# A third slot for the split weights of the first step behind three LayerNorms, and the order of work around it

## The chip, the cores and the metric

The kernel runs on one core of a Trainium2 chip. The metric is the device time of one execution in microseconds (us). The engines, as the profile names them, are PE (TensorE, matrix products; PEld is its weight load), DVE (VectorE), ACT (ScalarE), POOL (GpSimd) and SP (SyncE, which here only issues DMAs). Each engine runs its own instruction list in order, and semaphores join the lists.

## The reference

Two decoder layers on 512 tokens of width 1024. Each layer is a mixer and a gated MLP, each followed by a LayerNorm over the residual sum:

```python
for i in range(DEPTH):                       # DEPTH = 2
    if i % 2 == 0:
        m = even_mixer(x, w_qkv_ab[i // 2], w_o_ab[i // 2], cos, sin)
    else:
        m = odd_mixer(x, w_qkv_c[i // 2], w_o_c[i // 2])
    x = layer_norm(DEEPNORM_ALPHA * x + m, ln_mix_g[i], ln_mix_b[i])
    f = conv_ffn(x, w_up[i], conv_w[i], conv_b[i], w_down[i])
    x = layer_norm(DEEPNORM_ALPHA * x + f, ln_ffn_g[i], ln_ffn_b[i])
```

`even_mixer` and `odd_mixer` are two kinds of attention, each with a q/k/v product before and an output product behind it. `conv_ffn` is `u = h @ w_up` (1024 to 2 x 2816), a causal convolution of width 3, `silu(g) * val`, and `@ w_down` (2816 to 1024). All is float32.

## The kernel before

**Products in three parts.** Every large product is made from a high and a low part of both factors: hi x hi, hi x lo and lo x hi are added in a PSUM bank. ACT copies a rounded high part, and the low part is the difference. So each weight takes three operations: SP loads it into `w_raw`, ACT writes `w_hi` (`heads`, L267, or half a step at a time in `unit_heads`, L274), and POOL writes `w_lo = w_raw - w_hi` in two units (`rest`, L215).

**Weight steps.** The weights are a stream of 98 steps of 1 MB, 49 for each layer: 0 is q and k of the first attention position, 1 to 4 are v, 5 to 11 are q and k of the other positions, 12 to 15 the output product, 16 to 37 the MLP's first product, 38 to 48 its second. Step c uses slot c % 2 of `w_raw`, `w_hi` and `w_lo`. Hence ACT may write the high part of step c only when PE has finished step c - 2, which `heads` waits for on the semaphore `w_used`. POOL's end of step c (`lo_ready`) lets PE use it, and lets SP load step c + 2.

**A LayerNorm.** There are four, numbered i = 0 to 3; behind the first three comes a product that needs the result turned (transposed), with its columns along the partitions. The 512 tokens are four tiles t of 128 rows, and tile t owns the banks 2t and 2t + 1. PE ends the product in front tile by tile (`last_two`). For tile t, DVE adds the bank to the residual and takes the mean (`norm_sum`, L537, L542); ACT takes the variance (`norm_stats`, L290 to L296); DVE makes (x - mean) * gain in `ln_mul` (`norm_mul`, L553), four tiny operations on [128x1] (`norm_out`, L561, L564, L567, L569) and the result in `x` (L572), which raises `xn`. Then PE turns the tile with eight transposes (`turn_x`, L775) back into the tile's banks, ACT writes its high part (`xt_heads`, L283) and DVE its low part (`xt_rests`, L525), which raises `lo`.

**Who turns what, when.** PE turns tile 0 and tile 1 between the last four visits of the product in front. Tile 2 is turned after its end. Then `first_columns` runs the first step behind the LayerNorm: its two units on the tokens of tiles 0 and 1 (24 matmuls each), then `turn_x` of tile 3, then other work (`meanwhile`), then both units on tiles 2 and 3. The other work is the same half of the next step (`up_half`, i = 0 and 2), or one tile of the first v step, 12 matmuls (`v_meanwhile`, i = 1). Steps 16, 49 and 65 are the first ones behind LayerNorm 0, 1 and 2.

**Memory.** The buffers of the attention, of the MLP and of the LayerNorm lie in the same stretch, one over another, since they are not alive at once. ACT loads `tri` (a mask of the second layer's attention) behind LayerNorm 1.

The only loops in this part are the ones over steps far from the LayerNorms. The order is written out by hand on each engine.

## Time and profile before

| | us |
|---|---|
| median of 3 runs | 1278.67 |
| lowest, highest | 1278.08, 1280.11 |
| the profiled execution, whole time | 1279.5 |
| its span, first to last instruction | 1277.7 |
| PE busy in the span | 1225.5 |
| ACT, DVE, POOL busy | 506.8, 639.3, 548.0 |

The span and what lies around it make up the profiled execution's own time, which is 0.8 us above the median. Times below are counted from the start of the span. A row of the timeline gives start, duration, engine, line, operation, and out<-in; in brackets stand the idle time before it and who ended it. A matmul's duration is longer than the spacing of matmuls, which are pipelined.

### The profile page before, as it was taken

The page shows a single profiled execution, that of the slowest core. Times are in us where ns is not written, and L with a number is a line of the kernel's source. Part 1 is how long each engine was busy: PE and PEld are TensorE (multiplying, and loading weights), DVE is VectorE, ACT ScalarE, POOL GpSimd, SP SyncE. Part 2 cuts the span into 40 slices and gives each one's busy share as a digit, 9 for nine tenths or more (in the row PEclk, how much of TensorE's full clock was granted, in tenths as well). Part 3 has the DMA queues.
Part 4 walks back from the last instruction along what each step waited for, and adds up shares of the span by engine and source line. Part 5 has one row for each costly group of instructions (what it writes and reads, how often), then busy time and mean ns, then how long its engine had stood idle before and what let it go on. Part 6 is the DMA issues. An engine that isn't in the chain of part 4 may idle for free.

```text
span 1277.7 us, 17006 instructions
## 1 busy us (share of the span) xinstructions
PE 1225.5 (96%) x6224; PEld 1008.6 (79%) x6224; DVE 639.3 (50%) x1007; ACT 506.8 (40%) x749; POOL 548.0 (43%) x240
## 2 busy tenths in 40 slices
PE   7999998989999999999989999989899999999996
PEld 7877776779888888888778777768888888888885
DVE  2036565285566656522370465553676565552226
ACT  3236465344333333322232456643443333343222
POOL 5535353333444444455434333312364444444551
PEclk9999999989999999999989999999999999999998
DMA  7221222122222222222222111111222222222211
GB/s 287 99 84 58 90 69 81 66 92 107 92 91 88 93 96 98 99 98 98 99 101 100 66 66 66 48 52 66 100 99 98 98 98 98 98 98 99 98 66 66
DMA packets 19879, 117.25 MB, mean 92 GB/s; under 512 B 2433, under 2 KB 2817, under 8 KB 7425
## 3 DMA queue, kind: packets, MB, share of 16 engines
q1 hardware_dynamic: 18256, 112.21, 24.5%
q10 hardware_dynamic: 1584, 4.51, 1.0%
q8 instruction: 28, 0.46, 0.1%
q14 instruction: 11, 0.08, 0.0%
HBM read 110.41 MB, written 2.10 MB: 88 GB/s over the span
## 4 chain that ended last, share of the span: by engine, by line
PE 57%; issue 23%; POOL 10%; DVE 6%; ACT 3%; DMA 0%; POOLq 0%; ACTq 0%; SPq 0%; DVEq 0%
PE bank L829 32%; PE bank L799 18%; POOL w_lo L215 10%; PE bank L875 2%; PE bank L902 1%; PE bank L889 1%; DVE probs L677 1%; PE bank L959 1%; DVE x L572 1%; PE bank L940 1%; PE bank L948 1%; ACT w_hi L267 1%; PE bank L775 1%; DVE x L537 1%; DMA x<-x_in 0%
## 5 line engine op out<-in xcount | busy, mean ns | idle before, releaser
L215 POOL TENSOR_TENSOR w_lo<-w_raw,w_hi 128x1024 fp32r<-128x1024 f32 x196 | 504.3, 2596 | 634.8 <-ACT w_hi L267 577.2
L829 PE MATMUL bank<-xt_hi,w_hi 128*128 128x512 f32 (+1 forms) x1056 | 399.2, 378 | 1.7 <-ACT v_all L304 1.7
L829 PE MATMUL bank<-xt_lo,w_hi 128*128 128x512 f32 (+1 forms) x1056 | 398.8, 378 | 0.0
L829 PE MATMUL bank<-xt_hi,w_lo 128*128 128x512 f32 (+1 forms) x1056 | 394.7, 374 | 0.0
L267 ACT ACTIVATE w_hi<-w_raw 128x2048 fp32r<-128x2048 f32 x94 | 179.6, 1911 | 206.6 <-PE bank L799 206.6
L829 PEld LDWEIGHTS bank<-xt_hi,w_hi 128*128 128x128 f32 x1056 | 201.3, 191 | 38.8 <-ACT v_all L304 2.4
L829 PEld LDWEIGHTS bank<-xt_lo,w_hi 128*128 128x128 f32 x1056 | 201.1, 190 | 38.9 <-issue 4.8
L829 PEld LDWEIGHTS bank<-xt_hi,w_lo 128*128 128x128 f32 x1056 | 201.0, 190 | 33.6
L799 PE MATMUL bank<-w_hi,a_hi 128*128 128x512 f32 x480 | 151.7, 397 | 2.9 <-POOL w_lo L215 1.9
L799 PE MATMUL bank<-w_hi,a_lo 128*128 128x512 f32 x480 | 148.8, 391 | 0.0
L799 PE MATMUL bank<-w_lo,a_hi 128*128 128x512 f32 x480 | 148.6, 391 | 0.0
L751 DVE TENSOR_TENSOR a_lo<-h_all,a_hi 128x1024 fp32r<-128x1024 f32 x22 | 52.9, 2405 | 150.1 <-ACT a_hi L462 150.1
L743 DVE TENSOR_TENSOR h_all<-sig,cv 128x512 f32 (+1 forms) x44 | 119.1, 2706 | 6.1 <-DVE cv L733 0.2
L799 PEld LDWEIGHTS bank<-w_hi,a_hi 128*128 128x128 f32 x480 | 88.8, 188 | 25.1 <-POOL w_lo L215 4.3
L799 PEld LDWEIGHTS bank<-w_hi,a_lo 128*128 128x128 f32 x480 | 90.3, 188 | 19.3 <-issue 0.2
L799 PEld LDWEIGHTS bank<-w_lo,a_hi 128*128 128x128 f32 x480 | 90.3, 188 | 19.1
L471 ACT ACTIVATE cg<-bank,conv 128x512 f32<-128x512 f32 x44 | 34.2, 778 | 122.4 <-PE bank L829 122.1
L729 DVE SCALAR_TENSOR_TENSOR cv<-bank,conv,cv 128x511 f32<-128x511 f32 x44 | 33.0, 749 | 91.2 <-ACT cv L477 91.2
L477 ACT ACTIVATE cv<-bank,conv 128x512 f32<-128x512 f32 x44 | 34.2, 777 | 82.3 <-PE bank L829 82.2
L475 ACT ACTIVATE sig<-cg 128x512 f32<-128x512 f32 x44 | 27.8, 632 | 82.5 <-DVE cg L733 82.5
L729 DVE SCALAR_TENSOR_TENSOR cg<-bank,conv,cg 128x511 f32<-128x511 f32 x44 | 33.0, 749 | 46.0 <-ACT cg L471 46.0
L329 ACT ACTIVATE probs<-probs,sm 128x128 f32<-128x128 f32 (+3 forms) x64 | 35.4, 555 | 43.1 <-DVE sm L633 43.1
(87 smaller groups left out, 1159.5 us busy)
## 6 DMA issues: line engine op xcount, KB each, us to landing
w_raw<-w_stream SPq DMA_DIRECT2D x97, 1024.0 KB, 4.8
x<-x_in SPq DMA_DIRECT2D x4, 512.0 KB, 7.1
gain<-ln_in ACTq DMA_DIRECT2D x4, 512.0 KB, 4.1
shift<-ln_in ACTq DMA_DIRECT2D x4, 512.0 KB, 5.3
qs<-qc SPq DMA_DIRECT2D x16, 128.0 KB, 2.1
ks<-kc SPq DMA_DIRECT2D x16, 128.0 KB, 2.1
out<-x SPq DMA_DIRECT2D x4, 512.0 KB, 2.6
w_raw<-w_stream SPq DMA_DIRECT2D x2, 512.0 KB, 6.0
```

What stands on the lines that cost most here:

```text
L215: pool.tensor_tensor(w_lo[s][:, part], w_raw[s][:, part], w_hi[s][:, part].bitcast(F32), ALU.subtract).then_inc(lo_ready, 1)
L267: act.activation(w_hi[c % 2][:, :], w_raw[c % 2][:, :], ACT.Copy).then_inc(hi_ready, 2)
L329: act.activation(e, e, ACT.Exp, bias=m[:, 0:1], scale=-1.0, accum_out=m[:, 1:2]).then_inc(a["ex"], 1)
L471: act.activation(cg[s][:, :], bank[2 * s][:, :], ACT.Identity, bias=tap(l, f, 3), scale=tap(l, f, 2)).then_inc(u["cg"], 1)
L475: act.activation(sig[s][:, :], cg[s][:, :], ACT.Sigmoid).then_inc(u["sg"], 1)
L477: act.activation(cv[s][:, :], bank[2 * s + 1][:, :], ACT.Identity, bias=tap(l, f + KF, 3), scale=tap(l, f + KF, 2)).then_inc(u["cv"], 1)
L729: dve.scalar_tensor_tensor(out=acc[:, 1:S], in0=ps[:, 0:S - 1], scalar=tap(l, tile, 1), in1=acc[:, 1:S], op0=ALU.mult, op1=ALU.add).then_i ...
L743: dve.tensor_tensor(h_all[:, bass.ds(f, 1), :], sig[s][:, :].rearrange("p (a q) -> p a q", a=1), cv[s][:, :].rearrange("p (a q) -> p a q", ...
L751: dve.tensor_tensor(a_lo[:, k:k + 2, :], h_all[:, bass.ds(2 * j, 2), :], a_hi[:, k:k + 2, :].bitcast(F32), ALU.subtract).then_inc(DN[l]["a ...
L799: mm = pe.matmul(bank[2 * t + g][:, :], lhs, w[s][:, u * UNIT + g * HALF:u * UNIT + (g + 1) * HALF], start=first and n == 0, stop=end and ...
L829: mm = pe.matmul(out_bank[:, tok], w, m, start=n == 0, stop=n == len(todo) - 1)
L875: mm = pe.matmul(bank[2 + h][:, k * P:(k + 1) * P], qa[par][part, qi * P:(qi + 1) * P], ka[par][part, k * P:(k + 1) * P], start=True, stop ...
```

## The change

Three steps, 16, 49 and 65, get slot 2 of `w_hi` and `w_lo`; the others count on in slots 0 and 1 without them. `w_raw` keeps two slots. The new buffers `w_hi2` and `w_lo2` lie above the LayerNorm's buffers, over buffers of attention and MLP that are dead by then; `cg1`, `cv1` and `sig1` are moved up, and the load of `tri` is moved behind the use of step 49. On the engines: ACT writes the high part of these steps ahead of the LayerNorm's first statistics; DVE's `xt_rests` of tiles 0 and 1 come earlier; PE no longer turns tile 2 ahead of the first step behind, but after its first unit, and tile 3 one half unit later than before.

```diff
@@ -50,6 +50,14 @@
+AHEAD = (AT_UP, PER_LAYER, PER_LAYER + AT_UP)
...
+def slot(c):
+    return 2 if c in AHEAD else (c - sum(a < c for a in AHEAD)) % 2
@@ -101,13 +109,16 @@
-            cg = [sb(f"cg{s}", [P, S], stack=st) for s in range(2)]
-            cv = [sb(f"cv{s}", [P, S], stack=st) for s in range(2)]
-            sig = [sb(f"sig{s}", [P, S], stack=st) for s in range(2)]
+            cg, cv, sig = ([sb(f"{n}0", [P, S], stack=st)] for n in ("cg", "cv", "sig"))
+            sb("below_second", [P, S], stack=st)
+            for n, tiles in (("cg", cg), ("cv", cv), ("sig", sig)):
+                tiles.append(sb(f"{n}1", [P, S], stack=st))
...
+            w_hi.append(sb("w_hi2", [P, 2 * UNIT], F32R, stack=st))
+            w_lo.append(sb("w_lo2", [P, 2 * UNIT], F32R, stack=st))
@@ -212,8 +223,8 @@
-                    pool.tensor_tensor(w_lo[s][:, part], w_raw[s][:, part],
-                                       w_hi[s][:, part].bitcast(F32), ALU.subtract).then_inc(lo_ready, 1)
+                    pool.tensor_tensor(w_lo[slot(c)][:, part], w_raw[s][:, part],
+                                       w_hi[slot(c)][:, part].bitcast(F32), ALU.subtract).then_inc(lo_ready, 1)
@@ -251,9 +262,11 @@
-                with pool.Fori(0, (PER_LAYER - AT_UP) // 2) as it:
+                rest(b + AT_UP)
+                rest(b + AT_UP + 1)
+                with pool.Fori(0, (PER_LAYER - AT_UP - 2) // 2) as it:
...
-                        rest(b + AT_UP + j, it)
+                        rest(b + AT_UP + 2 + j, it)
@@ -264,14 +277,7 @@
-                act.activation(w_hi[c % 2][:, :], w_raw[c % 2][:, :], ACT.Copy).then_inc(hi_ready, 2)
...
-            def unit_heads(c, u):
...
-                act.wait_ge(raw_full[c % 2], filled(c, 0))
-                act.wait_ge(w_used, c - 1)
-                part = slice(u * UNIT, (u + 1) * UNIT)
-                act.activation(w_hi[c % 2][:, part], w_raw[c % 2][:, part], ACT.Copy).then_inc(hi_ready, 1)
+                act.activation(w_hi[slot(c)][:, :], w_raw[c % 2][:, :], ACT.Copy).then_inc(hi_ready, 2)
@@ -430,12 +436,11 @@
-                    act.wait_ge(N[1]["xn"], NT)
-                    act.dma_start(tri[:, :], tri_in).then_inc(tri_full, 16)
...
+                    act.dma_start(tri[:, :], tri_in).then_inc(tri_full, 16)
@@ -451,6 +456,7 @@
                     heads(b + AT_O + 2 + c)
+                heads(b + AT_UP, used=False)
                 for i, after in ((2 * l, b + AT_O + 4), (2 * l + 1, b + PER_LAYER)):
@@ -497,6 +503,8 @@
                                 chunk_heads(j + 2, it)
+                        if l < DEPTH - 1:
+                            heads(after, used=False)
                     if i == 2 * DEPTH - 1:
@@ -505,10 +513,9 @@
-                        unit_heads(after, 0)
...
-                        unit_heads(after, 1)
-                        heads(after + 1)
+                        act.wait_ge(w_used, after - 1)
+                        heads(after + 1, used=False)
@@ -581,11 +588,12 @@
                 norm_sum(i, 2)
+                if turn:
+                    xt_rests(i + 1, 0)
                 norm_mul(i, 2)
                 if turn:
-                    xt_rests(i + 1, 0)
+                    xt_rests(i + 1, 1)
                     norm_out(i, 2)
-                    xt_rests(i + 1, 1)
                     norm_sum(i, 3)
@@ -783,15 +791,15 @@
-                    c, it, slot = steps[m]
-                    s = c % 2
+                    c, it, at = steps[m]
+                    s = slot(c)
...
-                        hi = a[0][:, slot + u, t * P:(t + 1) * P]
-                        lo = a[1][:, slot + u, t * P:(t + 1) * P]
+                        hi = a[0][:, at + u, t * P:(t + 1) * P]
+                        lo = a[1][:, at + u, t * P:(t + 1) * P]
@@ -816,7 +824,7 @@
-                s = c % 2
+                s = slot(c)
@@ -840,9 +848,12 @@
                             pass
+                        if (half, unit) == (0, 0) and i > 0:
+                            turn_x(i, 2)
                     if half == 0 and i > 0:
+                        meanwhile(0)
                         turn_x(i, 3)
-                        meanwhile()
+                        meanwhile(1)
@@ -995,6 +1006,8 @@
                 def first_v(t, _):
+                    if t >= 2:
+                        pe.wait_ge(T[2 * l]["lo"], 2 * t + 2)
                     if t == 0:
@@ -1006,7 +1019,7 @@
-                def v_meanwhile():
+                def v_meanwhile(_):
@@ -1042,11 +1055,10 @@
-                turn_x(2 * l + 1, 2)
@@ -1054,17 +1066,17 @@
-                def up_half(half):
...
-                    for unit in range(2):
-                        for _ in col_unit(b + AT_UP + 1, 0, unit, bank[2 + unit], U[l]["g_mm"], half):
-                            pass
...
-                first_columns(b + AT_UP, 0, U[l]["g_mm"], 2 * l + 1, lambda: up_half(0))
-                up_half(1)
-                with pe.Fori(1, KF // 2) as it:
-                    up_body(0, it)
-                    up_body(1, it)
+                def up_half(half, unit):
...
+                    for _ in col_unit(b + AT_UP + 1, 0, unit, bank[2 + unit], U[l]["g_mm"], half):
+                        pass
...
+                first_columns(b + AT_UP, 0, U[l]["g_mm"], 2 * l + 1, lambda unit: up_half(0, unit))
+                up_half(1, 0)
+                up_half(1, 1)
+                with pe.Fori(0, KF // 2 - 1) as it:
+                    up_body(2, it)
+                    up_body(3, it)
@@ -1091,8 +1103,6 @@
-                if l < DEPTH - 1:
-                    turn_x(2 * l + 2, 2)
```

**ACT at the start of LayerNorm 0** (`w_hi0` is slot 0 of the high parts, `n0_` and `t1_` semaphores of LayerNorm 0 and of the turning behind it), before and then after:

```order
L267 ACTIVATE w_hi0<-w_raw0 128x2048 [waits w_used,raw_full0]
L267 ACTIVATE w_hi1<-w_raw1 128x2048 [waits w_used,raw_full1]
L290 ACTIVATE ln_junk,stat<-x,stat 128x1024 [waits n0_mean]
L293 ACTIVATE stat<-stat,eps 128x1 [waits n0_sq]
```

```order
L280 ACTIVATE w_hi0<-w_raw0 128x2048 [waits w_used,raw_full0]
L280 ACTIVATE w_hi1<-w_raw1 128x2048 [waits w_used,raw_full1]
L280 ACTIVATE w_hi2<-w_raw0 128x2048 [waits raw_full0]
L296 ACTIVATE ln_junk,stat<-x,stat 128x1024 [waits n0_mean]
L299 ACTIVATE stat<-stat,eps 128x1 [waits n0_sq]
```

The high part of step 16 now stands ahead of the first variance, in slot 2, and waits only for its load.

**ACT in the middle of LayerNorm 0**, from the variance of tile 2 on, before and then after:

```order
L290 ACTIVATE ln_junk,stat<-x,stat 128x1024 [waits n0_mean]
L293 ACTIVATE stat<-stat,eps 128x1 [waits n0_sq]
L296 ACTIVATE stat<-stat 128x1 [waits n0_lv]
L274 ACTIVATE w_hi0<-w_raw0 128x1024 [waits w_used,raw_full0]
L283 ACTIVATE xt_hi<-bank2 128x4x128 [waits t1_mm]
L283 ACTIVATE xt_hi<-bank3 128x4x128
L274 ACTIVATE w_hi0<-w_raw0 128x1024 [waits w_used,raw_full0]
L267 ACTIVATE w_hi1<-w_raw1 128x2048 [waits w_used,raw_full1]
```

```order
L296 ACTIVATE ln_junk,stat<-x,stat 128x1024 [waits n0_mean]
L299 ACTIVATE stat<-stat,eps 128x1 [waits n0_sq]
L302 ACTIVATE stat<-stat 128x1 [waits n0_lv]
L289 ACTIVATE xt_hi<-bank2 128x4x128 [waits t1_mm]
L289 ACTIVATE xt_hi<-bank3 128x4x128
L280 ACTIVATE w_hi0<-w_raw1 128x2048 [waits raw_full1,w_used]
```

The two half steps of 16 are gone; step 17 stays behind `xt_heads` of tile 1, as one whole step.

**DVE at the same place**, from the mean of tile 2 on, before and then after:

```order
L542 TENSOR_SCALAR stat<-stat 128x1 [waits n0_sum]
L553 SCALAR_TENSOR_TENSOR ln_mul<-x,stat,gain 128x1024 [waits n0_xn,n0_mean]
L525 TENSOR_TENSOR xt_lo<-bank0,xt_hi 128x4x128 [waits t1_hi]
L525 TENSOR_TENSOR xt_lo<-bank1,xt_hi 128x4x128
L561 TENSOR_SCALAR stat<-stat 128x1 [waits n0_sq]
L564 SCALAR_TENSOR_TENSOR stat<-stat 128x1 [waits n0_y0,n0_va]
L567 TENSOR_SCALAR stat<-stat 128x1 [waits n0_nt]
L569 TENSOR_TENSOR stat<-stat 128x1 [waits n0_nt]
L572 SCALAR_TENSOR_TENSOR x<-ln_mul,stat,shift 128x1024 [waits n0_mulg,n0_nt]
L525 TENSOR_TENSOR xt_lo<-bank2,xt_hi 128x4x128 [waits t1_hi]
L525 TENSOR_TENSOR xt_lo<-bank3,xt_hi 128x4x128
```

```order
L549 TENSOR_SCALAR stat<-stat 128x1 [waits n0_sum]
L532 TENSOR_TENSOR xt_lo<-bank0,xt_hi 128x4x128 [waits t1_hi]
L532 TENSOR_TENSOR xt_lo<-bank1,xt_hi 128x4x128
L560 SCALAR_TENSOR_TENSOR ln_mul<-x,stat,gain 128x1024 [waits n0_xn,n0_mean]
L532 TENSOR_TENSOR xt_lo<-bank2,xt_hi 128x4x128 [waits t1_hi]
L532 TENSOR_TENSOR xt_lo<-bank3,xt_hi 128x4x128
L568 TENSOR_SCALAR stat<-stat 128x1 [waits n0_sq]
L571 SCALAR_TENSOR_TENSOR stat<-stat 128x1 [waits n0_y0,n0_va]
L574 TENSOR_SCALAR stat<-stat 128x1 [waits n0_nt]
L576 TENSOR_TENSOR stat<-stat 128x1 [waits n0_nt]
L579 SCALAR_TENSOR_TENSOR x<-ln_mul,stat,shift 128x1024 [waits n0_mulg,n0_nt]
```

The low parts of tiles 0 and 1 (L525, now L532) both stand ahead of the four tiny operations and of the result of tile 2 (L572, now L579).

**PE at the end of step 15**, before, and then the two places after where step 16 begins and where tile 2 is turned:

```order
L799 MATMUL bank6<-w_hi1,a_lo 128x512
L799 MATMUL bank7<-w_hi1,a_lo 128x512
L775 MATMUL bank4<-ident,x 128x128 [waits n0_xn]
L775 MATMUL bank4<-ident,x 128x128 x3
L775 MATMUL bank5<-ident,x 128x128 x4
L829 MATMUL bank0<-xt_hi,w_hi0 128x256 [waits lo_ready,t1_lo]
L829 MATMUL bank0<-xt_lo,w_hi0 128x256
```

```order
L807 MATMUL bank6<-w_hi1,a_lo 128x512
L807 MATMUL bank7<-w_hi1,a_lo 128x512
L837 MATMUL bank0<-xt_hi,w_hi2 128x256 [waits lo_ready,t1_lo]
L837 MATMUL bank0<-xt_lo,w_hi2 128x256
L837 MATMUL bank0<-xt_hi,w_lo2 128x256
```

```order
L837 MATMUL bank0<-xt_lo,w_hi2 128x256
L837 MATMUL bank0<-xt_hi,w_lo2 128x256
L783 MATMUL bank4<-ident,x 128x128 [waits n0_xn]
L783 MATMUL bank4<-ident,x 128x128 x3
L783 MATMUL bank5<-ident,x 128x128 x4
L837 MATMUL bank1<-xt_hi,w_hi2 128x256 [waits lo_ready]
L837 MATMUL bank1<-xt_lo,w_hi2 128x256
```

Tile 2's turn (banks 4 and 5, waiting for `n0_xn`) has moved behind the 24 matmuls of the first unit (bank 0). Tile 3's turn (banks 6 and 7) moved likewise behind the first half unit of step 17.

## Rows read from the trace of the kernel before

**Rows 1.** The page: PE busy in the span, and the DMA issues of the weights.

```profile
PE 1225.5 (96%) x6224; PEld 1008.6 (79%) x6224; DVE 639.3 (50%) x1007; ACT 506.8 (40%) x749; POOL 548.0 (43%) x240
...
w_raw<-w_stream SPq DMA_DIRECT2D x97, 1024.0 KB, 4.8
```

**Rows 2.** PE's waits: engine line, waited for: us in total, times, longest.

```profile
PE bank L775 <- DVE x L572: 13.6, 3, 4.5
```

**Rows 3.** Timeline of PE at LayerNorm 0: start us, us, engine, line, operation.

```profile
273.74 0.62 PE L799 MATMUL bank<-w_lo,a_hi 128*128 128x512 f32 x2
274.19 0.61 PE L799 MATMUL bank<-w_hi,a_lo 128*128 128x512 f32 x2
279.31 1.97 PE L775 MATMUL bank<-ident,x 128*128 128x128 f32 x8 [4.51 <-DVE x L572]
...
288.40 1.03 PE L775 MATMUL bank<-ident,x 128*128 128x128 f32 x8
289.19 0.36 PE L829 MATMUL bank<-xt_hi,w_hi 128*128 128x256 f32 x1
289.39 0.28 PE L829 MATMUL bank<-xt_lo,w_hi 128*128 128x256 f32 x1
289.51 0.28 PE L829 MATMUL bank<-xt_hi,w_lo 128*128 128x256 f32 x1
```

**Rows 4.** Timeline of PE at LayerNorms 1 and 2, turns of tiles 2 and 3.

```profile
652.28 1.97 PE L775 MATMUL bank<-ident,x 128*128 128x128 f32 x8 [4.55 <-DVE x L572]
...
660.96 1.03 PE L775 MATMUL bank<-ident,x 128*128 128x128 f32 x8
...
901.80 1.40 PE L775 MATMUL bank<-ident,x 128*128 128x128 f32 x8 [4.50 <-DVE x L572]
...
910.10 1.04 PE L775 MATMUL bank<-ident,x 128*128 128x128 f32 x8
```

**Rows 5.** Timeline of DVE at LayerNorm 0.

```profile
260.99 1.28 DVE L553 SCALAR_TENSOR_TENSOR ln_mul<-x,stat,gain 128x1024 f32<-128x1024 f32 x1
...
271.86 1.28 DVE L525 TENSOR_TENSOR xt_lo<-bank,xt_hi 128x512 fp32r<-128x512 f32 x2
...
273.68 2.21 DVE L569 TENSOR_TENSOR stat<-stat 128x1 f32<-128x1 f32 x1
...
275.93 3.33 DVE L572 SCALAR_TENSOR_TENSOR x<-ln_mul,stat,shift 128x1024 f32<-128x1024 f32 x1
...
281.95 2.96 DVE L553 SCALAR_TENSOR_TENSOR ln_mul<-x,stat,gain 128x1024 f32<-128x1024 f32 x1
...
290.59 1.29 DVE L525 TENSOR_TENSOR xt_lo<-bank,xt_hi 128x512 fp32r<-128x512 f32 x2 [2.46 <-ACT xt_hi L283]
```

**Rows 6.** Timeline of ACT at LayerNorm 0.

```profile
272.38 1.04 ACT L274 ACTIVATE w_hi<-w_raw 128x1024 fp32r<-128x1024 f32 x1
273.32 1.06 ACT L283 ACTIVATE xt_hi<-bank 128x512 fp32r<-128x512 f32 x2
...
275.23 1.91 ACT L267 ACTIVATE w_hi<-w_raw 128x2048 fp32r<-128x2048 f32 x1
```

**Rows 7.** Timeline of POOL at LayerNorm 0, and at step 51.

```profile
252.88 4.75 POOL L215 TENSOR_TENSOR w_lo<-w_raw,w_hi 128x1024 fp32r<-128x1024 f32 x2 [3.41 <-ACT w_hi L267]
273.50 10.34 POOL L215 TENSOR_TENSOR w_lo<-w_raw,w_hi 128x1024 fp32r<-128x1024 f32 x4 [15.86 <-ACT w_hi L274]
...
673.04 4.73 POOL L215 TENSOR_TENSOR w_lo<-w_raw,w_hi 128x1024 fp32r<-128x1024 f32 x2 [16.25 <-ACT w_hi L267]
```

**Rows 8.** Stretches: length, busy us (instructions) of each engine, PE clock, DMA.

```profile
279.30:284.60 5.30, 5.29 (x25) 5.29 (x26) 5.23 (x8) 2.58 (x6) 4.53 (x2) 0.50 0.54 198
...
844.40:847.80 3.40, 3.40 (x10) 2.62 (x9) 2.42 (x5) 1.61 (x4) 0.69 (x1) 0.50 0.41 116
...
850.10:854.00 3.90, 2.32 (x14) 2.07 (x15) 3.80 (x6) 1.65 (x4) 0.00 (x0) 1.00 0.00 0
```

**Rows 9.** Timeline of PE: waits of the odd attention ahead of two stretches of rows 8.

```profile
843.66 0.33 PE L948 MATMUL bank<-ident,probs 128*128 128x128 f32 x1 [2.48 <-ACT probs L380]
...
851.68 0.55 PE L948 MATMUL bank<-ident,probs 128*128 128x128 f32 x3 [1.59 <-ACT probs L380]
```

## The prediction

> **What bounds the kernel now.** The page comes first: PE is busy 1225.5 of 1277.7 us [rows 1], so a gain must come from PE's idle time or from its clock. PE's waits come next. The longest entry is the turning of tiles (L775), which waits three times for DVE's LayerNorm result (L572), 13.6 us in all [rows 2]: 4.51 us at LayerNorm 0 [rows 3], 4.55 and 4.50 at LayerNorms 1 and 2 [rows 4]. Each is the turn of tile 2, placed where PE has nothing else to do.
>
> The timeline then shows two things behind these waits. First, a wait costs a little more than its idle time: matmuls are issued every 0.227 us (rows of two, 0.45 apart), so PE could have issued again at 274.19 + 0.45 = 274.64 but issued at 279.31 [rows 3]. That is 4.67, or idle + 0.16; for the others 4.71 and 4.66. Second, the clock: the granted clock stands at 0.50, the lower level of 1.2 GHz, right behind the wait [rows 8]. From the turn of tile 2 to that of tile 3 PE has 8 transposes (288.40 to 289.19 = 0.79) and 48 matmuls (0.12 each, 289.39 to 289.51), 6.55 us at full clock; it took 288.40 - 279.31 = 9.09 [rows 3], 8.68 and 8.30 [rows 4]. The clock cost 2.54, 2.13 and 1.75. Together: 14.04 + 6.42 = **20.5 us** stand behind these three turns.
>
> Why does L572 come so late? POOL subtracts steps 16 and 17 from 273.50 to 283.84 [rows 7]. While it runs, DVE's operations with two inputs in SBUF stand: L569 on [128x1] takes 2.21 us, L572 takes 3.33 where 1.28 is its usual time (as that of L553 at 260.99), L553 at 281.95 takes 2.96 and ends 1.07 behind POOL's last subtraction [rows 5, 7]. L569 caught the first subtraction (2.38 us each, half of 4.75) and L572 the second.
>
> **The change, part by part,** at LayerNorm 0; the other two run the same pattern.
>
> *The high part of step 16 goes first.* Its load is issued when the subtraction of step 14 ends (ahead of 252.88) and lands 4.8 us later [rows 1], long before POOL is free at 252.88 + 4.75 = 257.63 [rows 7]. So POOL subtracts step 16 from 257.6 to 262.35. That meets L553 of tile 0, issued at 260.99: it ends at 262.35 + 1.07 = 263.42, not 262.27. DVE's chain is **late by 1.15 us** from there. PE doesn't feel it at the turns of tiles 0 and 1, which by my reading stand 1.6 and 1.9 us behind their results in the trace.
>
> *The first unit no longer waits for tile 2.* It needs both low parts of tiles 0 and 1. ACT's variance of tile 2 ended for its next operation at 272.38 [rows 6]; 1.15 later is 273.53. There stands now `xt_heads` of tile 1, with no half step ahead of it: done 1.06 later, 274.59 [rows 6]. DVE follows in 0.04 and takes 1.29 for the low part [rows 5]: 275.92; PE issues at about 275.96. Lost: 275.96 - 274.64 = **1.32 us**. DVE reaches that point with 0.4 us to spare, so its new order costs nothing.
>
> *Tile 2 is turned after 24 matmuls.* PE is ready at 275.96 + 24 x 0.12 = 278.84. When is `x` there? L569 starts 1.82 us behind the first subtraction of a low part (271.86 to 273.68 [rows 5]), at 274.63 + 1.82 = 276.45; L572 is due 0.2 us later. On ACT the high part of step 17 starts 0.95 behind `xt_heads` (273.32 to 274.28, by its own length less the overlap), at 274.48, takes 1.91 [rows 6] and POOL starts 0.08 behind it (273.42 to 273.50), at **276.47**. So L569 and POOL start within 0.02 us of each other, which my arithmetic can't separate. Two answers:
> - DVE is first. L569 is through at once, POOL takes over at about 276.6 and L572 stands for one subtraction: 276.6 + 2.38 + 1.07 = 280.05. PE issues at 280.10, lost **1.26**.
> - POOL is first, as in the trace. L569 stands until 278.85, L572 until 281.2, and ends at 282.27. PE issues at 282.32, lost **3.48**.
>
> I take the first: by the sum DVE is 0.02 us ahead. In both, POOL has 2 subtractions there, not 4.
>
> *Tile 3 is turned after two more half units.* PE gets there at 280.10 + 0.79 + 48 x 0.12 = 286.65. L553 of tile 3 meets the second subtraction (to about 282.4), ends at 283.5, and L572 about 2.0 us later, 285.5. No wait, 1.1 us to spare. The low part of tile 3 is done 3.48 us after the turn begins (288.40 to 290.59 + 1.29 [rows 3, 5]); the cover was two half units and is now one: 0.79 + 24 x 0.12 = 3.67 us. It holds by 0.15 us, so I cost it at nothing; with 12 matmuls of a v tile at LayerNorm 1 the cover is 3.51, even. If the cover is gone, it costs the lateness one for one, under 0.5 us.
>
> *One new wait, at step 51.* Behind LayerNorm 1 three tiles of the first v step (8.2 us) stood between the end of step 49 and step 51; now two (5.45 us), since one went into the cover. ACT still starts step 51 only when step 49 is used, though slot 1 is free sooner, and POOL ends it at 673.04 + 4.73 = 677.77 [rows 7]. PE's half of step 49 ends at about 670.36, so its second unit is due at 670.36 + 5.45 + 1.36 = 677.17: lost 0.6, **0.65 us** with the hand-over. It could be 0 if the halves slip, and at most 2.7, the work that moved.
>
> *Loads, `tri`, slots.* SP may load step 18 at 262.4, much earlier than before, into a queue that is idle there. `tri` is needed 30 us after its new place. Slots 0 and 1 serve steps as far apart as before. Nothing here.
>
> **The clock.** No row shows two waits of 1.2 us so close. The nearest: behind a wait of 1.59 us the clock stays at 1.00, behind one of 2.48 us it stands at 0.50 [rows 8, 9]. Single waits of 1.1 us are nearer to the first, both together (2.3 idle) nearer to the second. Bounds: 0, and 2.54, 2.13, 1.75 as now. I take 0, as each wait is followed by 24 matmuls without a gap.
>
> **The sum.** Before 20.5. After 3 x (1.32 + 1.26) + 0.65 = 8.4. Gain 12.1 us: 1279.5, the profiled execution's time, becomes 1267.4; against the median, 0.8 lower, **1266.6**.
>
> **The rivals.**
> 1. *Two short waits, and the clock falls as before.* Adds 6.4: 1273.0. For it: 2.3 us idle within 5.
> 2. *POOL first, double block.* 3 x (1.32 + 3.48) + 0.65 = 15.05, and the clock falls as before, 6.42: 21.5 against 20.5, so 1279.7. For it: a margin of 0.02 us, and that all three LayerNorms show this order today. The gain is then eaten by the 1.15 and by waits that only moved.
> 3. *L572 slips in as well.* L572 is due 0.04 us behind L569's end. If it is in first, it ends at 276.65 + 1.28 = 277.93, before PE is ready: 3 x 1.32 + 0.65 = 4.6, 1262.8. Against it: POOL's third subtraction was held by L572 (10.34 us for four, 0.8 more than 4 x 2.38), and resumed with no gap that I can see; a waiting POOL took over between L569 and L572. The Trainium skill, SBUF — State Buffer, "A bandwidth-pool intuition that's wrong", has a blocked GpSimd resume about 115 ns after DVE ends; by that rule L572 would be in first and the time would be this one.
> 4. *Slower: the clock stays low for longer.* Double block as in 2, but the low clock runs over both waits and what lies between, twice the loss of now (12.8): 6.4 more, 1286. It decides once the three low stretches cost over 8 us together, 2.7 each; LayerNorm 0 stands at 2.54 today.
> 5. *The early subtraction doesn't happen,* because step 16's load or high part is late: then POOL's four subtractions stay in the middle and the time about 1279. Against: 3 us between landing and POOL's being free.
>
> Beside rivals 2 and 3: the trace shows that the one that is there first holds the other up for its whole operation (L572, 3.33 us). The Trainium skill says the same in SBUF — State Buffer, "SBUF: two separate sides": the shared port pair is an exclusive lock for "whichever … starts first". By that rule and the 0.02 us the time would be the forecast; it also speaks against this change, as it puts one more POOL step against the LayerNorm's first tile.
>
> **How the numbers follow.** Forecast 0.42; rival 1 0.14; rival 2 0.25; rival 3 0.07; rival 4 0.08; rival 5 0.04. A measurement of this kernel tells 0.2%, 2.6 us, from no change. Faster: 0.42 + 0.14 + 0.07 = 0.63. Slower: rival 4 and the upper edge of 2, 0.11. Same: 0.26. The range leaves out rivals 3 and 4: 1264 (forecast less the 0.65 and some of the waits) to 1281.5 (rival 2 with 2 us of clock). Most of the chance has one sign, yet the range must reach over no change.
>
> **What would show it.** L553 of tile 0 at about 2.4 us, not 1.28. PE's waits for L525 of 1.2 us and for L572 of about 1.0 us (or 3.3) at each LayerNorm, instead of 4.5. POOL one step of 4.75 us ahead and one in the middle. L569 at 0.16 or 2.2 us, which alone tells forecast from rival 2. Clock 1.00 or 0.50 behind the waits. A wait of PE for POOL of 0.6 us near step 51. I am wrong if POOL meets DVE elsewhere, or if PE's cover for tile 3 is short.

## The result, and the profile after

| | us |
|---|---|
| kernel before, median of 4 runs beside it | 1279.16 (1278.08 to 1280.11) |
| kernel after, median of 4 runs | 1268.04 (1266.48 to 1268.33) |
| ratio, 95% interval | 0.991 (0.990 to 0.992) |
| profiled execution of after, its span | 1268.13, 1266.2 |

The change makes the kernel 11.1 us (0.9%) faster; the forecast was 1266.6 us. The page shows first that PE does the same work in less time: 6224 matmuls as in [rows 1], busy 5.9 us less. These 5.9 us go with the clock; the other 5.6 of the span's 11.5 (1277.7 less 1266.2) are idle time.

```profile
PE 1219.6 (96%) x6224; PEld 1001.3 (79%) x6224; DVE 632.5 (50%) x1007; ACT 507.0 (40%) x746; POOL 548.3 (43%) x240
```

PE's waits (engine line, waited for: us in total, times, longest). L783, L837, L807 are L775, L829, L799 of before; L579 and L532 are L572 and L525. The 13.6 us of [rows 2] have become 3.1. In their place stand 3.7 us for the low part of tile 1. The waits for POOL were 1.9 us, 3 times, in before; the fourth, at step 51, is new:

```profile
PE bank L837 <- DVE xt_lo L532: 3.7, 3, 1.2
PE bank L783 <- DVE x L579: 3.1, 3, 1.0
PE bank L807 <- POOL w_lo L226: 2.6, 4, 0.8
```

PE's timeline has two short waits at each LayerNorm, here at LayerNorms 0, 1 and 2, where [rows 3, 4] had one of 4.5 us. The last row is step 51:

```profile
276.77 0.39 PE L837 MATMUL bank<-xt_hi,w_hi 128*128 128x256 f32 x1 [1.24 <-DVE xt_lo L532]
...
280.82 1.09 PE L783 MATMUL bank<-ident,x 128*128 128x128 f32 x8 [1.05 <-DVE x L579]
...
645.08 0.38 PE L837 MATMUL bank<-xt_hi,w_hi 128*128 128x256 f32 x1 [1.21 <-DVE xt_lo L532]
...
649.12 1.09 PE L783 MATMUL bank<-ident,x 128*128 128x128 f32 x8 [1.03 <-DVE x L579]
...
890.97 0.39 PE L837 MATMUL bank<-xt_hi,w_hi 128*128 128x256 f32 x1 [1.21 <-DVE xt_lo L532]
...
895.02 1.09 PE L783 MATMUL bank<-ident,x 128*128 128x128 f32 x8 [1.05 <-DVE x L579]
...
672.39 0.73 PE L807 MATMUL bank<-w_hi,xt_hi 128*128 128x512 f32 x2 [0.70 <-POOL w_lo L226]
```

DVE and POOL at LayerNorm 0 show who met whom. The product with the gain of tile 0 (L560) now takes 2.46 us, since POOL's early subtraction is there. L576 of tile 2 starts 0.014 us ahead of POOL (277.255 and 277.269 before rounding), and is through in 0.16 us. L579 then stands for one subtraction and takes 3.31 us:

```profile
261.76 2.46 DVE L560 SCALAR_TENSOR_TENSOR ln_mul<-x,stat,gain 128x1024 f32<-128x1024 f32 x1
...
277.25 0.16 DVE L576 TENSOR_TENSOR stat<-stat 128x1 f32<-128x1 f32 x1
277.45 3.31 DVE L579 SCALAR_TENSOR_TENSOR x<-ln_mul,stat,shift 128x1024 f32<-128x1024 f32 x1
```

```profile
253.66 9.47 POOL L226 TENSOR_TENSOR w_lo<-w_raw,w_hi 128x1024 fp32r<-128x1024 f32 x4 [3.41 <-ACT w_hi L280]
...
277.27 5.75 POOL L226 TENSOR_TENSOR w_lo<-w_raw,w_hi 128x1024 fp32r<-128x1024 f32 x2 [14.13 <-ACT w_hi L280]
```

The stretches (length, busy us and instructions of PE, PEld, DVE, ACT, POOL, then PE clock and DMA) show the clock at 1.00, the upper level of 2.4 GHz, behind the second wait; the same stretch of before stood at 0.50 [rows 8]:

```profile
279.30:284.60 5.30, 4.25 (x38) 4.06 (x37) 5.16 (x10) 2.27 (x6) 3.72 (x2) 1.00 0.11 20
```

### The profile page after: what moved, and what is told of

The parts are those of the page before. It is cut to its first block, busy times and chain, and to the rows that moved or that the text cites. A ratio compares the mean times of both kernels' runs of the same rounds, so it can differ in the third digit from the quotient of the medians.

```text
span 1266.2 us, 17008 instructions
## 1 busy us (share of the span) xinstructions
PE 1219.6 (96%) x6224; PEld 1001.3 (79%) x6224; DVE 632.5 (50%) x1007; ACT 507.0 (40%) x746; POOL 548.3 (43%) x240
## 4 chain that ended last, share of the span: by engine, by line
PE 57%; issue 23%; POOL 10%; DVE 5%; ACT 3%; DMA 1%; POOLq 0%; SPq 0%; ACTq 0%; DVEq 0%
PE bank L837 31%; PE bank L807 18%; POOL w_lo L226 10%; PE bank L886 2%; PE bank L913 1%; PE bank L900 1%; DVE probs L685 1%; PE bank L970 1%; DVE x L579 1%; PE bank L951 1%; ACT w_hi L280 1%; PE bank L959 1%; DVE x L544 1%; DMA x<-x_in 1%; DVE ln_mul L560 0%
## 5 line engine op out<-in xcount | busy, mean ns | idle before, releaser
L837 PE MATMUL bank<-xt_hi,w_hi 128*128 128x512 f32 (+1 forms) x1056 | 397.1, 376 | 5.3 <-DVE xt_lo L532 3.7
L837 PE MATMUL bank<-xt_lo,w_hi 128*128 128x512 f32 (+1 forms) x1056 | 396.6, 376 | 0.0
L837 PE MATMUL bank<-xt_hi,w_lo 128*128 128x512 f32 (+1 forms) x1056 | 392.7, 372 | 0.0
L280 ACT ACTIVATE w_hi<-w_raw 128x2048 fp32r<-128x2048 f32 x97 | 185.4, 1911 | 209.1 <-PE bank L807 204.6
L837 PEld LDWEIGHTS bank<-xt_hi,w_hi 128*128 128x128 f32 x1056 | 198.8, 188 | 43.3 <-DVE xt_lo L532 5.1
L837 PEld LDWEIGHTS bank<-xt_lo,w_hi 128*128 128x128 f32 x1056 | 198.7, 188 | 39.3 <-issue 4.8
L837 PEld LDWEIGHTS bank<-xt_hi,w_lo 128*128 128x128 f32 x1056 | 198.7, 188 | 33.4
L807 PE MATMUL bank<-w_hi,a_hi 128*128 128x512 f32 x480 | 151.9, 397 | 2.9 <-POOL w_lo L226 1.9
L807 PE MATMUL bank<-w_lo,a_hi 128*128 128x512 f32 x480 | 148.5, 391 | 0.0
L807 PE MATMUL bank<-w_hi,a_lo 128*128 128x512 f32 x480 | 148.3, 390 | 0.0
L807 PEld LDWEIGHTS bank<-w_hi,a_hi 128*128 128x128 f32 x480 | 89.0, 188 | 25.4 <-POOL w_lo L226 4.3
L807 PEld LDWEIGHTS bank<-w_lo,a_hi 128*128 128x128 f32 x480 | 90.3, 188 | 19.1
L807 PEld LDWEIGHTS bank<-w_hi,a_lo 128*128 128x128 f32 x480 | 90.1, 188 | 19.1 <-issue 0.2
```

The lines of the kernel that those rows point to most:

```text
L280: act.activation(w_hi[slot(c)][:, :], w_raw[c % 2][:, :], ACT.Copy).then_inc(hi_ready, 2)
L807: mm = pe.matmul(bank[2 * t + g][:, :], lhs, w[s][:, u * UNIT + g * HALF:u * UNIT + (g + 1) * HALF], start=first and n == 0, stop=end and ...
L837: mm = pe.matmul(out_bank[:, tok], w, m, start=n == 0, stop=n == len(todo) - 1)
```

## The experiments

The theory: the time is set by which of DVE's operations with two inputs in SBUF POOL's subtractions meet, and by PE's clock behind the waits. The rivals: the new orders on PE and DVE bring the gain; or the outcome of the 0.014 us is worth little. The experiments ran in three groups, each with runs of before beside it, and a ratio is against those: 1278.4 us for slot_only, order_only, old_dve and dve_late, 1277.9 for dve_later, gate_first, gate_second and gate_all, and 1279.0 for dve_chained, gate_all51 and slot_gates. The `N`, `xn` and `w_used` of the edits are the semaphores told of ahead.

### The slot alone: slot_only

The new slot and the early high part stay; PE's and DVE's orders are those of before.

```diff
                 norm_sum(i, 2)
-                if turn:
-                    xt_rests(i + 1, 0)
                 norm_mul(i, 2)
                 if turn:
-                    xt_rests(i + 1, 1)
+                    xt_rests(i + 1, 0)
                     norm_out(i, 2)
+                    xt_rests(i + 1, 1)
...
+                turn_x(2 * l + 1, 2)
...
-                first_columns(b + AT_UP, 0, U[l]["g_mm"], 2 * l + 1, lambda unit: up_half(0, unit))
+                first_columns(b + AT_UP, 0, U[l]["g_mm"], 2 * l + 1, lambda: (up_half(0, 0), up_half(0, 1)))
```

> The changed kernel with the old orders of PE and DVE: only the third slot, the early high part and the early subtraction of steps 16, 49 and 65 are left, and PE turns tile 2 right behind the product in front. By my sums at LayerNorm 0: DVE late by 1.15 us at tile 0; L572 of tile 2 now starts about 1.4 us ahead of POOL's next step, so it isn't blocked, and PE waits 1.7 us for it, then 0.4 for the low part of tile 1, then 1.1 for tile 3 (its first pass is blocked by POOL instead). 3.2 us lost at each LayerNorm against 2.3 to 2.6 in the changed kernel, and no wait at step 51: 1269 to 1270, if the clock stays up. The rival, that the new orders of PE and DVE bring the gain and the slot only makes room for them: then this run stays near the kernel before, 1276 or more, with waits of 4 us.

Measured: 1268.06 us, ratio 0.992 (0.990 to 0.993), 1 us less than expected. The slot alone has the same median as the whole change. PE has two waits at each LayerNorm here too, but both for L579, of tile 2 (1.57, 1.67, 1.60) and of tile 3 (0.89, 0.88, 1.08), and none at step 51. The page of PE's waits and DVE's timeline:

```profile
PE bank L782 <- DVE x L579: 7.7, 6, 1.7
```

```profile
275.25 1.28 DVE L579 SCALAR_TENSOR_TENSOR x<-ln_mul,stat,shift 128x1024 f32<-128x1024 f32 x1
...
276.46 1.28 DVE L532 TENSOR_TENSOR xt_lo<-bank,xt_hi 128x512 fp32r<-128x512 f32 x2
...
279.23 3.29 DVE L560 SCALAR_TENSOR_TENSOR ln_mul<-x,stat,gain 128x1024 f32<-128x1024 f32 x1
```

In this order L579 of tile 2 starts 1.4 us ahead of POOL (276.69), and meets nothing. The low part (L532), with one input in a PSUM bank, runs under POOL's subtraction in its usual 1.28 us. POOL's second subtraction holds L560 of tile 3 instead. So the orders trade a block at tile 2 for one at tile 3, at nearly the same price, and the old orders don't need the 0.014 us.

The equal medians hide a little. From the end of the product ahead of LayerNorm 0 to the end of the span slot_only took 991.1 us and after 990.7; dve_later below, which has after's orders, took 990.5. By these traces the new orders are worth 0.4 to 0.6 us, and after's median lacks it: three of its four executions had a mean clock of 0.993, those of slot_only 0.995 or 0.996. The part on what the sum missed says where that comes from.

### The orders alone: order_only

Before, with the new orders of PE and DVE and two slots.

```diff
                 norm_sum(i, 2)
+                if turn:
+                    xt_rests(i + 1, 0)
                 norm_mul(i, 2)
                 if turn:
-                    xt_rests(i + 1, 0)
+                    xt_rests(i + 1, 1)
                     norm_out(i, 2)
-                    xt_rests(i + 1, 1)
...
+                        if (half, unit) == (0, 0) and i > 0:
+                            turn_x(i, 2)
...
```

> The kernel before with the new orders of PE and DVE and its two slots: POOL's four subtractions stay in the middle of the LayerNorm. My sum at each LayerNorm: the first unit waits 1.3 us for the low parts, as in the changed kernel; then L572 of tile 2 is blocked behind two subtractions and PE waits 2.9 us more, 4.2 in all against 4.7 before. With the clock up behind it about 1272; with it down as before about 1278. The rival, that the orders bring the gain: 1270 or less.

Measured: 1287.73 us, ratio 1.007 (1.005 to 1.009), slower than before and outside what was expected. PE and DVE at LayerNorm 0:

```profile
276.74 0.36 PE L830 MATMUL bank<-xt_hi,w_hi 128*128 128x256 f32 x1 [1.26 <-POOL w_lo L215]
...
284.71 1.97 PE L776 MATMUL bank<-ident,x 128*128 128x128 f32 x8 [4.86 <-DVE x L572]
```

```profile
276.51 2.45 DVE L564 SCALAR_TENSOR_TENSOR stat<-stat 128x1 f32<-128x1 f32 x1
...
279.19 2.10 DVE L569 TENSOR_TENSOR stat<-stat 128x1 f32<-128x1 f32 x1
281.32 3.33 DVE L572 SCALAR_TENSOR_TENSOR x<-ln_mul,stat,shift 128x1024 f32<-128x1024 f32 x1
```

My sum had two blocked operations, L569 and L572. The trace has three: the new order moved L564, also on [128x1] with two inputs, under POOL as well. The wait is 4.86 us at LayerNorms 0 and 1 and 4.87 at 2, behind one of 1.24 to 1.26, and the clock behind it is 0.50 to 0.52 at all three. The first wait is as long as I expected, but for another reason: the low part was ready at 276.42, and PE waited for POOL's first subtraction, which ended at 276.59. So the orders without the slot are a loss, and the rival that they bring the gain is out.

### PE's order without DVE's: old_dve

After, with DVE's three lines as in slot_only. L579 and the low part of tile 1 change places.

> The changed kernel with DVE's old order alone (low part of tile 1 behind the result of tile 2). PE's two waits of 1.2 and 1.0 us at each LayerNorm become one of about 2.8 us, ahead of the first unit, and none at the turn of tile 2, since L572 is then ahead of POOL. By the waits alone 0.4 us more at each LayerNorm, 1269. If one wait of 2.8 us lets the clock fall where two of 1.1 us don't, 1.7 to 2.5 us more at each: 1274 to 1276. The rival, that the clock fell before for another reason than the length of the wait, says 1269.

Measured: 1271.61 us, ratio 0.994 (0.993 to 0.996), between the two answers. There is one wait at each LayerNorm:

```profile
PE bank L836 <- DVE xt_lo L532: 8.4, 3, 2.8
```

The idle time, 8.4 us, is 1.6 more than the 3.7 and 3.1 of after. The clock fell behind it at LayerNorms 0 and 2 and not at 1: idle time and clock together, old_dve lost 1.8, 0.4 and 2.1 us on after at the three, and the 0.4 is no more than the longer wait. The stretch behind the wait at LayerNorm 0:

```profile
277.50:281.00 3.50, 3.50 (x17) 3.50 (x18) 3.43 (x6) 1.74 (x4) 3.50 (x2) 0.52 0.00 0
```

With PE's new order, then, DVE's is needed: it is worth 3.6 us by the medians, 1.6 of it idle time and the rest clock.

### Moving the arrival by a tenth of a microsecond: dve_late, dve_later, dve_chained

Each puts a small write ahead of tile 2's tiny operations or between them, to bring L576 behind POOL's start. In dve_late it is one column ahead of the first of them:

```diff
+                if t == 2 and i < 2 * DEPTH - 1:
+                    dve.memset(stat[:, t, 9:10], 0.0)
```

> The changed kernel with one more tiny DVE operation (a memset of an unused [128x1]) ahead of the four tiny ones of tile 2 at LayerNorms 0, 1 and 2. It costs DVE under 0.1 us by itself, but POOL's subtraction, 0.014 us behind L576 now, is then ahead of it. If the one that is first holds the other up for its whole operation, L576 takes 2.2 us, L579 3.3, and PE's wait at the turn of tile 2 grows from 1.0 to 3.2 us: 6 to 7 us more, 1274 to 1275, and with the clock down behind it 1278 to 1281. If the order of arrival didn't matter, the time stays at 1268.

Measured: 1267.83 us, ratio 0.991, as after. L576 still started 0.003 us ahead of POOL and took 0.16 us: the write ran beside the first of the tiny operations. In dve_later it is `dve.memset(pad[:, :], 0.0)` on 96 columns, ahead of the wait for `nt`:

> The changed kernel with one DVE memset of 96 columns of an unused buffer just ahead of L576 of tile 2 at LayerNorms 0 to 2, some 0.15 us. The memset tried before was absorbed: L576 still started 0.003 us ahead of POOL and ran through. This one puts it about 0.14 us behind POOL. Theory (the one that is first holds the pair for its whole operation): L576 takes about 2.2 us and L579 3.3, PE's wait at the turn of tile 2 grows from 1.0 to about 3.3 us at each LayerNorm, and the clock falls behind it: 6.6 us for the waits, up to 6 for the clock, 1275 to 1281. Rival (the order of arrival is not what decides): 1268.

Measured: 1266.97 us, ratio 0.992; L576 at 276.409, POOL at 276.424. Absorbed again, so neither run tests anything but that such a filler can vanish in a wait. In dve_chained DVE waits for its own write:

```diff
+                if t == 2 and i < 2 * DEPTH - 1:
+                    dve.memset(pad[:, :], 0.0).then_inc(pad_set, 1)
+                    dve.wait_ge(pad_set, i + 1)
                 dve.wait_ge(n["nt"], 3 * t + 2)
```

> As the run with the memset of 96 columns, but L576 now waits for the memset by a semaphore. There the memset ran beside DVE's own hand-over and L576 still started 0.015 us ahead of POOL. This should put L576 about 0.1 us behind POOL. Theory (the one that is first holds the pair for its whole operation): L576 2.2 us, L579 3.3 us, PE's wait at the turn of tile 2 from 1.0 to 3.3 us, the clock down behind it: 1274 to 1281. Rival (order of arrival doesn't decide): the time stays at 1267 to 1268.

Measured: 1278.21 us, median of 10 runs, ratio 1.000 (0.999 to 1.001): no gain is left. By themselves the write and its wait cost 0.1 us: L576 (here L581) starts 0.29 us behind the start of the tiny operation L574, in after 0.19 us. But it now starts 0.09 us behind POOL, and the timelines of DVE and POOL show the double block:

```profile
276.35 2.33 DVE L581 TENSOR_TENSOR stat<-stat 128x1 f32<-128x1 f32 x1
...
278.71 3.33 DVE L584 SCALAR_TENSOR_TENSOR x<-ln_mul,stat,shift 128x1024 f32<-128x1024 f32 x1
```

```profile
276.26 4.70 POOL L228 TENSOR_TENSOR w_lo<-w_raw,w_hi 128x1024 fp32r<-128x1024 f32 x2 [14.13 <-ACT w_hi L282]
```

```profile
PE bank L788 <- DVE x L584: 9.7, 3, 3.2
...
PE bank L842 <- DVE xt_lo L534: 3.9, 3, 1.3
```

The waits are 6.8 us longer than in after. The stretches behind them, at LayerNorms 0, 1 and 2, show the clock held at the first and at 0.50, 1.2 GHz, at the other two:

```profile
282.10:285.00 2.90, 2.90 (x25) 2.90 (x26) 2.80 (x7) 1.43 (x3) 0.00 (x0) 1.00 0.92 328
...
652.70:655.00 2.30, 2.30 (x11) 2.30 (x12) 2.23 (x6) 0.86 (x1) 0.00 (x0) 0.50 1.01 306
...
902.20:905.00 2.80, 2.80 (x14) 2.80 (x15) 2.73 (x7) 1.38 (x3) 0.00 (x0) 0.50 0.91 328
```

The start of one operation of 0.16 us, a tenth of a microsecond later at each LayerNorm, decides 10 us of the kernel's time: 6.8 are waits, the rest is nearly all clock. The mechanism is that of rival 2; its size would have been 1279.7, with the clock down at all three.

### Placing POOL: gate_first, gate_second, gate_all, gate_all51

If the blocks are the cause, POOL's subtractions need only be kept off DVE's operations with two SBUF inputs. In gate_all POOL waits at three places (`i` is the LayerNorm, `c` its first step behind):

```diff
+            for i, c in enumerate(AHEAD):
+                gate[c, 1] = (i, 2)
+                gate[c + 1, 0] = (i, 3)
+                if i != 1:
+                    gate[c + 1, 1] = (i, 4)
...
                 for u in range(2):
+                    if isinstance(it, int) and (c, u) in gate:
+                        i, t = gate[c, u]
+                        pool.wait_ge(N[i]["xn"], t)
```

gate_first has only the first line of the loop: the second half of step 16 is subtracted once tile 1's result is there, that is, behind L579 of tile 1.

> The changed kernel with one more wait on POOL: the second subtraction of steps 16, 49 and 65 waits until x of tile 1 is written (xn at 2), where DVE has no operation with two SBUF inputs for 2.6 us. Theory: the block of L560 at tile 0 goes (2.46 us to 1.28) and with it the 1.15 us by which all of DVE is late; PE's first wait falls from 1.2 to nearly nothing, the second stays at 1.0: 3.5 us less, 1264.5. Rival (the first wait comes from ACT's and DVE's order, not from the early subtraction): 1268.

Measured: 1263.92 us, ratio 0.989 (0.987 to 0.991). L560 of tile 0 (here L566) is at its usual time again, the wait for the low part is gone and the one for `x` is left:

```profile
260.87 1.28 DVE L566 SCALAR_TENSOR_TENSOR ln_mul<-x,stat,gain 128x1024 f32<-128x1024 f32 x1
```

```profile
PE bank L789 <- DVE x L585: 2.9, 3, 1.0
```

gate_second has only the second line: step 17's first half waits for tile 2's result.

> The changed kernel with one more wait on POOL: the first subtraction of the second step behind each LayerNorm (17, 50, 66) waits until x of tile 2 is written (xn at 3). Theory: L579 of tile 2 takes 1.28 us, not 3.3, and PE's wait of 1.0 at its turn goes; POOL then meets L560 of tile 3 and one tiny operation, so that tile 3's turn waits 0.1 to 0.5. 2.4 to 3.5 us less: 1264.5 to 1265.6. Rival: the wait only moves to tile 3, 1268.

Measured: 1265.73 us, ratio 0.990 (0.989 to 0.992), 0.1 above what was expected. The other wait is the one left:

```profile
PE bank L843 <- DVE xt_lo L538: 3.8, 3, 1.3
```

Here L576 and POOL no longer meet, so nothing hangs on the 0.014 us. gate_all has all three:

> Both waits, and the second subtraction of steps 17 and 66 waits until x of tile 3 is written (step 50's doesn't, since PE needs it sooner). Theory: the two gains add up and the meeting at tile 3 goes at LayerNorms 0 and 2. PE loses 0.2 to 0.5 us at each LayerNorm besides step 51: 6.5 to 7.2 us less than the changed kernel, 1261 to 1261.5. Rival: POOL, held back, is late for PE at the second unit of step 17 (ready 1 us before it is needed by my sum): 1264 or more.

Measured: 1260.97 us, ratio 0.987 (0.985 to 0.989). PE waits at the LayerNorms for nothing over 0.12 us, and for POOL at step 51 as after. At LayerNorm 0 POOL's three subtractions are each released by DVE's `x` (L588):

```profile
268.95 2.41 POOL L235 TENSOR_TENSOR w_lo<-w_raw,w_hi 128x1024 fp32r<-128x1024 f32 x1 [9.25 <-DVE x L588]
...
276.57 2.40 POOL L235 TENSOR_TENSOR w_lo<-w_raw,w_hi 128x1024 fp32r<-128x1024 f32 x1 [5.21 <-DVE x L588]
...
282.15 2.40 POOL L235 TENSOR_TENSOR w_lo<-w_raw,w_hi 128x1024 fp32r<-128x1024 f32 x1 [3.19 <-DVE x L588]
```

Not every block is gone. The subtraction at 276.57 still meets tile 3's product with the gain (here L569), at all three LayerNorms, and at LayerNorm 1 step 50's second one also holds an operation of tile 3 on [128x1], for 2.18 us. Neither costs PE anything, because tile 3's turn comes later than the result:

```profile
277.99 2.06 DVE L569 SCALAR_TENSOR_TENSOR ln_mul<-x,stat,gain 128x1024 f32<-128x1024 f32 x1
```

gate_all51 also starts step 51's high part earlier, behind `qa`:

```diff
                     act.activation(qa[0][:, :], bank[0][:, :], ACT.Copy, scale=SB_SCALE).then_inc(a["q_ok"], 1)
+                    act.wait_ge(w_used, b)
+                    heads(b + 2, used=False)
                     act.wait_ge(w_used, b + 1)
...
-                for c in range(2, AT_QK + 2):
+                for c in range(2 + l, AT_QK + 2):
```

> The kernel with all three waits on POOL (1261.0), and ACT writes the high part of step 51 as soon as step 48 is used and the q columns are taken, not only when step 49 is used: slot 1 is free then, since step 49 has slot 2. The wait of PE for POOL at step 51 (0.70 us) goes: 1260.3. The rival, that step 51's subtraction then meets something else: 1261.

Measured: 1260.68 us, ratio 0.986 (0.984 to 0.987), against a before of 1279.0. The wait at step 51 is gone from the trace. The time differs from gate_all's (1260.05 to 1262.28) by less than their runs spread, so the 0.7 us is seen as a wait and not as time. These two are the fastest kernels of the study: 17.0 us (1.3%) and 18.3 us (1.4%) below the before beside them.

### Placed POOL with the old orders: slot_gates

The edits of slot_only and gate_all together.

> The slot with the old orders of PE and DVE, and the three waits on POOL. With the slot alone the old orders were as fast as the new ones. With POOL out of the way: PE waits 0.6 us for tile 2, 0.4 for the low part of tile 1, nothing for tile 3, and nothing at step 51; the new orders wait 0.2 and 0.7 once. So the new orders are worth 3 x 0.8 - 0.7 = 1.7 us here: 1262.5 to 1263. The rival, that the orders are worth nothing at all: 1261.

Measured: 1264.9 us, ratio 0.989 (0.987 to 0.991), 2 us more than expected. PE still waits 1.2 us for tile 2 at each LayerNorm, and 1.03 for tile 3 at LayerNorm 1. POOL and DVE at LayerNorm 0 show why:

```profile
270.04 2.39 POOL L235 TENSOR_TENSOR w_lo<-w_raw,w_hi 128x1024 fp32r<-128x1024 f32 x1 [9.24 <-DVE x L588]
```

```profile
271.45 2.06 DVE L569 SCALAR_TENSOR_TENSOR ln_mul<-x,stat,gain 128x1024 f32<-128x1024 f32 x1
```

In the old order tile 2's product with the gain comes ahead of tile 0's low part, and meets the delayed subtraction; in the new one the low part, with one input in PSUM, stands there. DVE's new order opens the hole into which POOL's step fits. Against gate_all51, which ran beside it, the new orders are worth 4.2 us; gate_all51 also has the edit for step 51, without which the new orders would wait 0.7 us there. Without the waits on POOL they are worth 0.4 to 0.6 us.

## Why the prediction was right

- **The early subtraction, DVE late by 1.15.** L560 of tile 0 was forecast at about 2.4 us and took 2.46; gate_first took the early meeting away and the wait behind it went too.
- **The first unit's wait.** Forecast loss 1.32 a time; measured idle 1.24, 1.21, 1.21, plus the hand-over of 0.16.
- **Tile 2's turn.** Forecast 1.26; measured 1.05, 1.03, 1.05 and the hand-over. The order on which it rests, DVE 0.02 ahead of POOL, was 0.014 ahead. At LayerNorm 1 it was 0.017.
- **Tile 3's turn and its low part.** Forecast no wait; PE has none there. The cover of 3.67 us held, by 0.2 us at LayerNorm 0 (low part done at 290.86, needed at about 291.05).
- **Step 51.** Forecast 0.65; idle 0.70.
- **The clock.** Forecast no loss; it stayed at 1.00. The choice between one wait and two as the nearer row, made without a row of two, held. dve_chained and old_dve show how near the other side is.

Stretch by stretch, the time that PE took from the end of one product to the end of the next one ahead of a LayerNorm fell by 4.59 us (372.93 to 368.34) from LayerNorm 0 to 1, by 3.68 from 1 to 2 and by 3.91 from 2 to the end. The forecast has 4.63, 3.61 and 3.83 for them: one LayerNorm's terms each, less the step 51 in the second as its place behind LayerNorm 1 asks. Their sum is 12.2 us, against 12.1.

**What the sum missed** lies ahead of LayerNorm 0. PE reached it 0.73 us later than before (product's end at 275.53 against 274.80), through code that the change leaves as it was. Behind a wait of 2.5 us in the attention, at 210 to 213 us, the clock stayed low longer. The same stretch in after, and in before:

```profile
216.50:219.50 3.00, 3.00 (x22) 2.09 (x18) 0.68 (x7) 0.75 (x4) 0.00 (x0) 0.72 0.03 5
```

```profile
216.50:219.50 3.00, 3.00 (x31) 2.12 (x26) 1.03 (x9) 1.30 (x6) 0.00 (x0) 1.00 0.03 5
```

That is the gap between 12.1 and the 11.4 of the two profiled executions (1279.5 and 1268.1). It seems to go with the execution and not with the change: order_only, which up to there is the kernel before, reached LayerNorm 0 at 275.48, and of the kernels with after's code up to there dve_later, old_dve and slot_only did at 274.62, 274.71 and 275.02, slot_gates and gate_second at 275.56 and 275.60. The fastest run of after, 1266.48, had a mean clock of 0.996 where the others had 0.993, and is 0.1 from the forecast. What makes an execution take one or the other wasn't tested. So whether the forecast is off by 0.1 or by 1.4 us is a matter of luck; the sum itself is borne out by the three stretches.

**What was right for a reason too thin.** The first answer was taken over rival 2 by 0.02 us of arithmetic. It came out, but the starts it was worked out from carry errors of that size, and a chance of 0.42 against 0.25 was all it could bear. The prediction also treated the change as one piece; slot_only shows that one half has nearly all of the gain, and order_only that the other half alone is a loss. My expectations of order_only (three operations blocked, not two) and slot_gates (which operation stands at POOL's new place) failed on the same step: I followed the operations that had been blocked before, and not the first one with two SBUF inputs that the new order brings under POOL.

**The rivals.** Rival 1 (clock falls) did not happen in after, and did in 2 of 3 places each in old_dve and dve_chained, with longer waits. Rival 2's mechanism and most of its size are shown by dve_chained. Rival 3 (L579 slips in) did not happen: POOL was in ahead of L579, although L579 came only 0.04 us behind L576's end. The Trainium skill (SBUF — State Buffer, "A bandwidth-pool intuition that's wrong") gives a resume of about 115 ns behind DVE's end, measured there on a DMA whose descriptors GpSimd writes; by it L579 would have been in first. No run here shows that gap: POOL's first subtraction took 2.413 us, no more than 0.03 over its usual 2.38 to 2.41, and the second, which L579 held up, ended 2.26 us behind L579, sooner than its own length. Rival 4's threshold of 8 us was passed by order_only alone (some 8.4 us, an estimate from its stretches between the LayerNorms less the waits), where the waits were longer still. Rival 5 is out by POOL's row at 253.66.

**Open.** When an operation asks for its turn against the other engine isn't recorded, only its start. Ahead by 0.014 us L576 won; L564 of order_only, 0.025 ahead of POOL's second subtraction but within the last 0.08 us of the first, lost. Nor is it shown that L576 held POOL up at all in after: by POOL's 2.413 us it was held for 0.03 us at most, so L576 may just have been through before POOL needed its turn. How far behind POOL it may start and still pass lies between 0.002 us ahead (dve_late) and 0.09 behind (dve_chained). The profiles of dve_late, dve_later and gate_first, other builds taken on two chips, have it 0.002 to 0.025 us ahead at every LayerNorm; nothing shows that it stays so elsewhere.

## What to carry to other kernels

List, for DVE, every operation with two inputs in SBUF, tiny ones included, and lay GpSimd's long ones over that list: each meeting can cost what is left of the GpSimd operation, and queued ones can block several in a row. Rather than trusting who comes first, let GpSimd wait for a semaphore that places it where DVE reads PSUM or has one input, or where the block is not on PE's path; here three such waits took the gain from 11 to 17 us. A slot that lets an engine work earlier is worth most when the order around it has been looked at with it, and each half should be timed alone.

## What the runs showed that was not expected

- An operation on one column, 0.16 us alone, took 2.1 to 2.45 us under GpSimd's subtraction of 2.38 us; with its start 0.09 us behind GpSimd's instead of 0.014 ahead (dve_chained) the gain of 0.9% was gone.
- A small write put ahead of a waiting operation of DVE (dve_late, dve_later) didn't move it: it started 0.003 and 0.015 us ahead of GpSimd, in after 0.014. Only where DVE waited for the write did the start move.
- The granted clock of TensorE stayed at 1.00 behind two waits of 1.2 and 1.05 us with 24 matmuls between them, at all three LayerNorms. Behind one wait of 2.8 us it fell at two of three, and behind 1.3 and 3.2 us likewise at two of three: the same wait at the same kind of place gives either.
